# Sliding attention: the shift is added on the way to SBUF, and four exponentials become one

## The reference

```python
def swa_sink_attention(q, k, v, sinks):
    ...
    s = jnp.einsum('bcqhgd,bckhd->bchgqk', qc, kb, preferred_element_type=F32) * (D ** -0.5)
    s = jnp.where(valid[None, :, None, None, None, :], s, -jnp.inf)
    sink = sinks.astype(F32).reshape(1, 1, Hkv, G, 1, 1)
    m = jnp.maximum(jnp.max(s, axis=-1, keepdims=True), sink)
    e = jnp.exp(s - m)
    p = e / (jnp.sum(e, axis=-1, keepdims=True) + jnp.exp(sink - m))
    out = jnp.einsum('bchgqk,bckhd->bcqhgd', p.astype(v.dtype), vb)
    return out.reshape(B, S, Hq * D)
```

## Time and profile before

| what | value |
|---|---|
| median of 3 runs | 2261.44 us (2260.76 to 2262.36) |
| the profiled execution | 2261.36 us, its span 2259.6 us |
| mean granted clock of TensorE | 0.998 |
| busy share of the span | TensorE 99%, weight loads 83%, VectorE 78%, ScalarE 52%, GpSimd 37% |
| the stage with the 32 groups | about 1430 to 1600 us of the span |

### The profile page before, as it was taken

The page is one execution under the profiler, slowest core; times in us unless marked ns, Lnnn a source line. Parts: engine busy times, 40 slices in busy tenths (PEclk is TensorE's granted clock), DMA queues, the critical chain, the costliest instruction groups (busy, mean ns, idle before and its releaser), DMA issues. The chain is left out here.

```text
span 2259.6 us, 31830 instructions
## 1 busy us (share of the span) xinstructions
PE 2227.7 (99%) x11331; PEld 1885.4 (83%) x11331; DVE 1761.6 (78%) x2696; ACT 1183.0 (52%) x1951; POOL 840.1 (37%) x750
## 2 busy tenths in 40 slices
PE   7999999999999999999999999999999999999999
PEld 6888889999888888888888888888888888888887
DVE  5886789956557888888799767756598888888987
ACT  5658888766433444444445644655444444444454
POOL 3113346310001677777400022222048777871000
PEclk9999999999999999999999999999999999999999
DMA  5111100100322122222663542411322222228435
GB/s 169 36 50 47 34 33 29 39 1 1 140 103 75 66 84 84 84 84 84 222 216 103 181 139 61 107 39 57 112 66 84 84 84 82 82 70 303 154 118 199
DMA packets 190504, 215.18 MB, mean 95 GB/s; under 512 B 15524, under 2 KB 136708, under 8 KB 190348
## 3 DMA queue, kind: packets, MB, share of 16 engines
q1 hardware_dynamic: 185052, 195.81, 27.3%
q10 hardware_dynamic: 5296, 17.34, 2.0%
HBM read 170.77 MB, written 39.98 MB: 93 GB/s over the span
## 5 line engine op out<-in xcount | busy, mean ns | idle before, releaser
L123 PE MATMUL trunk_ps<-l_bhi,l_ahi 128*128 128x512 f32 x528 | 206.0, 390 | 0.5 <-DVE l_blo L3082 0.4
L123 PE MATMUL trunk_ps<-l_bhi,l_alo 128*128 128x512 f32 x528 | 205.5, 389 | 0.0
L123 PE MATMUL trunk_ps<-l_blo,l_ahi 128*128 128x512 f32 x528 | 205.4, 389 | 0.0
L123 PE MATMUL trunk_ps<-l_t_hi,l_s_hi 128*128 128x512 f32 x456 | 177.4, 389 | 0.0
L123 PE MATMUL trunk_ps<-l_t_hi,l_s_lo 128*128 128x512 f32 x456 | 177.4, 389 | 0.0
L123 PE MATMUL trunk_ps<-l_t_lo,l_s_hi 128*128 128x512 f32 x456 | 177.4, 389 | 0.0
L2698 POOL TENSOR_TENSOR l_s_lo<-l_raw,l_s_hi 128x512 fp32r<-128x512 f32 x90 | 158.1, 1765 | 45.5 <-ACT l_s_hi L2607 45.5
L2476 ACT ACTIVATE l_ahi<-l_a 128x512 fp32r<-128x512 f32 x132 | 83.2, 631 | 159.7 <-PE trunk_ps L123 151.2
L2698 POOL TENSOR_TENSOR l_s_lo<-l_w_sum,l_s_hi 128x512 fp32r<-128x512 f32 x76 | 120.4, 1586 | 56.6 <-ACT l_s_hi L2607 56.4
L216 POOL TENSOR_TENSOR wring_w_lo<-wring_raw,wring_w_hi 128x256 fp32r<-128x256 f32 x72 | 56.6, 817 | 191.8 <-ACT wring_w_hi L211 191.8
L123 PE MATMUL trunk_ps<-rest_hi,l_s_hi 128*128 128x512 f32 x304 | 118.3, 389 | 0.0
(11 more groups left out here) (495 smaller groups left out, 6722.6 us busy)
## 6 DMA issues: line engine op xcount, KB each, us to landing
l_draw<-in_ffn_w_out SPq DMA_DIRECT2D x154, 256.0 KB, 2.8
l_raw<-in_ffn_w_in SPq DMA_DIRECT2D x48, 512.0 KB, 4.6
gated_dram<-l_gate_out SPq DMA_DIRECT2D x44, 512.0 KB, 2.6
l_a<-gated_dram SPq DMA_DIRECT2D x88, 256.0 KB, 4.2
wring_raw<-in_even_w_in SPq DMA_DIRECT2D x20, 512.0 KB, 3.9
l_raw_g<-in_ffn_w_in SPq DMA_DIRECT2D x20, 512.0 KB, 3.9
l_raw_v<-in_ffn_w_in SPq DMA_DIRECT2D x20, 512.0 KB, 4.9
l_wt<-in_ffn_w_out SPq DMA_DIRECT2D x22, 256.0 KB, 6.0
```

The lines of the kernel that those rows point to most:

```text
L123: mm = pe.matmul(o, w, m, start=a, stop=z, skip_group_check=onto)
```

## The change

VectorE no longer leaves the scores in PSUM. Behind the shift it does one more operation in each group: scores + shift, for all four pairs at once, from S[n % 2] into prob[n % 2] (new semaphore `moved`). For that the shift is kept in the scores' own scale: `nbias` is now the smaller of -maximum and -8 x sink, with the new row `nsink8`, made by two small operations at the start. The exponent of the sink becomes 0.125 x nbias + sink, again one operation. ScalarE waits for `moved` and takes all four blocks' exponentials in one operation, prob into prob, with scale 0.125. Scores wait for `moved` where they waited for `exp_done`, and so does the feed-forward part's first product. The wait for `T_ready`, which guards prob, goes from ScalarE's exp to VectorE's move.

```diff
@@ -1084,13 +1086,8 @@
         def exp(n):
             nk = self.keys_of(self.where(n)[1])
-            sc.wait_ge(self.nb_ready, n + 1)
-            if n >= 2:
-                sc.wait_ge(self.T_ready, n - 1)
-            for u in range(self.PAIRS):
-                ins = sc.activation(self.prob[n % 2][:, u, 0:nk], self.S[n % 2][:, u * P:u * P + nk], ACT.Exp,
-                                    bias=self.nbias[:, n % self.ROWS, u:u + 1], scale=0.125)
-            ins.then_inc(self.exp_done, 1)
+            sc.wait_ge(self.moved, n + 1)
+            sc.activation(self.prob[n % 2][:, :, 0:nk], self.prob[n % 2][:, :, 0:nk], ACT.Exp, scale=0.125).then_inc(self.exp_done, 1)
@@ -1263,7 +1260,7 @@
             if n >= 2:
-                pe.wait_ge(self.exp_done, n - 1)
+                pe.wait_ge(self.moved, n - 1)
@@ -1381,13 +1378,18 @@
             dve.wait_ge(self.mx_ready, n + 1)
-            dve.scalar_tensor_tensor(out=self.nbias[:, n % self.ROWS, :], in0=self.mx[:, n % self.ROWS, :], scalar=-0.125,
-                                     in1=self.nsink[:, self.PAIRS * kv:self.PAIRS * kv + self.PAIRS], op0=ALU.mult, op1=ALU.min).then_inc(self.nb_ready, 1)
+            row, pairs, nk = n % self.ROWS, slice(self.PAIRS * kv, self.PAIRS * kv + self.PAIRS), self.keys_of(c)
+            dve.scalar_tensor_tensor(out=self.nbias[:, row, :], in0=self.mx[:, row, :], scalar=-1.0, in1=self.nsink8[:, pairs],
+                                     op0=ALU.mult, op1=ALU.min).then_inc(self.nb_ready, 1)
             dve.wait_ge(self.nb_ready, n + 1)
+            if n >= 2:
+                dve.wait_ge(self.T_ready, n - 1)
+            dve.tensor_tensor(self.prob[n % 2][:, :, 0:nk], self.S[n % 2].rearrange("p (u k) -> p u k", u=self.PAIRS)[:, :, 0:nk],
+                              self.nbias[:, row, :].rearrange("p (u c) -> p u c", c=1).to_broadcast([P, self.PAIRS, nk]), ALU.add).then_inc(self.moved, 1)
             if n >= self.ROWS:
                 dve.wait_ge(self.es_done, n - self.ROWS + 1)
-            dve.tensor_tensor(self.arg[:, n % self.ROWS, :], self.nbias[:, n % self.ROWS, :],
-                              self.nsink[:, self.PAIRS * kv:self.PAIRS * kv + self.PAIRS], ALU.subtract).then_inc(self.arg_ready, 1)
+            dve.scalar_tensor_tensor(out=self.arg[:, row, :], in0=self.nbias[:, row, :], scalar=0.125, in1=self.nsink[:, pairs],
+                                     op0=ALU.mult, op1=ALU.subtract).then_inc(self.arg_ready, 1)
@@ -1446,12 +1448,13 @@
             dve.tensor_scalar(self.nsink[half, :], self.sink[half, :, s], -1.0, None, ALU.mult).then_inc(self.sink_ready, 1)
+            dve.tensor_scalar(self.nsink8[half, :], self.sink[half, :, s], -8.0, None, ALU.mult).then_inc(self.sink_ready, 1)
...
-        dve.wait_ge(self.sink_ready, 2)
+        dve.wait_ge(self.sink_ready, 4)
@@ -2872,7 +2875,7 @@
-                    pe.wait_ge(odd.exp_done, odd.NG)
+                    pe.wait_ge(odd.moved, odd.NG)
```

More of the change, by code:

```diff
@@ L938, in __init__ @@
             at(x, [P] + rows, F32, small + 96 + 128 * i) for i, x in enumerate(("mx", "nbias", "arg", "es", "den", "inv")))
+        self.nsink8 = at("nsink8", [P, 8], F32, small + 864)
         self.ss, self.var, self.rstd = stats
@@ L956, in __init__ @@
             st.sem(x) for x in ("S_ready", "mx_ready", "nb_ready", "arg_ready", "exp_done", "es_done"))
+        self.moved = st.sem("moved")
         self.T_ready, self.copied, self.O_ready, self.den_ready, self.inv_ready, self.O_taken = (
```

## The result

The changed kernel takes 2269.64 us (median of six executions, 2263.76 to 2271.26), against 2261.02 (2259.51 to 2262.36) for the kernel before on the same chip: a ratio of 1.0035, with a 95% interval of 1.0022 to 1.0048. That is slower, and above the range of 2261.3 to 2266.4. The six executions are not alike. One took 2263.76, with a mean granted clock of 0.998, which is the forecast to 0.04 us; that close a hit is luck, since the six executions of the kernel before lie 2.85 us apart. The other five took 2269.04 to 2271.26, at 0.994 or 0.995. The profiled one is of the second kind: 2269.82 us, span 2268.0, mean clock 0.994.

The account below looks back on a forecast made before the run. TensorE, busy in 99% of the span, was taken to bound the kernel, with waits only in the sliding attention's head. Head delays of 0.8 + 1.1 + 0.5 = 2.4 us on 2261.4 gave 2263.8 us, range 2261.3 to 2266.4.

Parts of the forecast that it names:

- Step 1: Head, last queries: VectorE's moves of groups 0 and 1 delay the query packing and so scores 2; +0.8 us.
- Step 2: Head, group 2: VectorE's wait for the turned block delays the values' copy and TensorE's first product with them; +1.1 us.
- Step 3: Slots 3 to 5, no mixing between groups yet: longer path to the exponentials makes TensorE's turns late; +0.5 us.
- 2 us more of TensorE idle in the head: Sign in the profile after: less than this much added TensorE idle would show Step 3 failing.
- From slot 5 on, nothing: Later slots: mixing gives 3.1 us of cover against a 0.3 longer path; VectorE's load rises to 74%; no time added.
- The costs of single operations: Per group: VectorE's move taken at 0.69 us, ScalarE's joined exponential at 0.71 us against 1.14 for four.
- The sum of 2.4: Total shift from the head and slots 3 to 5: 0.8 + 1.1 + 0.5 us, giving 2263.8 us.
- the clock falls: Rival, head: TensorE's new holes lower the granted clock, costing 1.7 us more, 2265.5 us; chance 0.09.
- The long move: Rival, mainly head: VectorE's move doubles to 1.28 us, adding 3.0 us, 2266.8 us; chance 0.08.
- A head that swallows the shift: Rival, head: most of the delay vanishes, 2262.2 us, or 2260.5 at best; chance 0.10.
- The quicker stretch: Rival, TensorE's long stretch: it becomes quicker as ScalarE reads PSUM less beside it; chance 0.03.
- A granted clock below 1.00 around 1440 to 1450: Sign in the profile after, in the head, that would show the forecast wrong.

Follow-up runs that it names:

- own buffer: Changed kernel with a separate probability buffer for group 2, so VectorE's move need not wait for group 0's turn: 2263.04 us, ratio 1.0005.
- v_first: Changed kernel with VectorE's copies of the values placed ahead of group 2's maximum, shift and move: 2263.25 us, ratio 1.0005.
- second profile: Changed kernel, unaltered, in a second set of runs: median 2268.49 us, ratio 1.0029; the profiled execution took 2264.70 us.
- best order: Changed kernel with group 1's maximum, shift and move behind the last query packing, and values' copies earlier on VectorE and ScalarE: 2262.18 us, ratio 1.0000.
- four exponentials in place: v_first with four exponentials in SBUF, one per pair, instead of one for all four pairs: 2265.21 us, ratio 1.0011.

## Why the prediction was wrong, point by point

- **Step 1 (+0.8): right.** Measured +0.72. The packing of the last queries starts later by group 1's move, and scores 2 start at 1439.64, forecast 1439.6. It has a neighbour that I had left out, and that the change doesn't make: where the swapped rows landed later, the hole was 1.79 instead of 1.02.
- **Step 2 (+1.1): right.** Measured +1.21, through the wait named (VectorE 1.57 us for the turn, forecast about 1.5) and the product at 1444.73 (forecast 1444.55). The own buffer and v_first each took away that wait, and with it the 1.21.
- **Step 3 (+0.5): right in its place, a little large.** Measured +0.29 to +0.33 where the clock did not fall (11.54 to 11.58, against 11.25). The exponential was a mis-sized term, 0.63 us where 0.71 was taken. Group 3 shows it alone: from the start of its shift to its turn it takes 1.61 us (1448.58 to 1450.19, second profile), and 1.39 before (1445.60 to 1446.99), so +0.22 for a forecast +0.30. TensorE waits 0.61 us for group 4, and no longer for group 5, where the kernel before had 0.38 and 0.55; how the rest of the 0.2 divides was not taken apart. As a sign I had set 2 us more of TensorE idle in the head. The second profile has holes of 4.2 us (1.79, 1.45, 0.19, 0.61, 0.16), 2.7 more than the 1.47 of the earlier trace rows, but 0.8 of that is the late swapped rows; the first has only 2.47, as at the low clock TensorE no longer waits for the exponentials. The sign was a poor one.
- **From slot 5 on, nothing: right.** TensorE's waits in the kernel after, from 1436 to 1620 us (line, releaser: us in total, times, longest), are the two of the head and one at 1610 us, which the kernel before has too (at 1601.5):

```profile
PE trunk_ps L1292 <- DVE odd_v_even L1467: 1.4, 1, 1.4
PE trunk_ps L1267 <- DVE odd_q L142: 1.0, 1, 1.0
PE trunk_ps L123 <- ACT main_cos L1123: 0.8, 1, 0.8
```

  With the clock back, a slot is still 5.40 us. TensorE's turns, and VectorE's heaviest slot, the one with the norm, in the timeline of the kernel after (compare):

```profile
1509.46 0.62 PE L1279 MATMUL trunk_ps<-main_const,odd_prob 128*128 128x128 f32 x4
...
1514.86 0.62 PE L1279 MATMUL trunk_ps<-main_const,odd_prob 128*128 128x128 f32 x4
...
1509.66 0.69 DVE L1378 TENSOR_REDUCE odd_mx<-trunk_ps 128x4 f32<-128x512 f32 x1 [1.89 <-PE trunk_ps L1268]
...
1515.08 0.68 DVE L1378 TENSOR_REDUCE odd_mx<-trunk_ps 128x4 f32<-128x512 f32 x1
```

  That slot of VectorE takes 5.42 us from maximum to maximum (forecast 5.6), without a gap, and pushes nobody. VectorE was busy 70% of the stretch, forecast 74%: in a row of dense operations the next one starts 0.61 us behind a move (1511.22 behind 1510.61), so a move costs 0.61 there, not 0.69, and the kernel after comes to this stretch some 7.6 us later than before. The own buffer's stretch, with no long fall ahead of it, has 99.09 of 138, 72%.
- **The costs of single operations.** Move 0.691 us x30, forecast 0.69. Exponential 0.631, forecast 0.71. The Trainium skill (VectorE: DVE Perf Modes, section "The TRN2 errata") gave an estimated 0.61 for the latter; the trace has 0.63, closer to the page than my row was, and that row of 0.71 has a per-partition operand that this exponential no longer has. Since nothing from slot 5 on waits for it, the difference is worth little.
- **The sum of 2.4: right for what it added up.** The three steps come to 2.2 us where the clock is 1.00. The two executions at 0.998 took 2263.76 and 2264.70, forecast 2263.8, but of the two only the second was profiled, and its head was 3.0 us longer, not 2.2. That the times agree so well is in part luck.
- **The clock: this is the step that failed.** The sum of 2.4 had it at nothing, and the rival "the clock falls" had it wrong in its chance and in its price. I gave it 0.09. In 10 of the 14 executions of the changed kernel the mean clock was 0.995 or less. What I held against it, the 1.47 us of holes in today's head at a clock of 1.00, adds up holes of 0.24 to 0.55 us each, and none is near the 1.5 us that I had myself forecast. The one row on such a single hole, a longer one of 1.94 us, showed a fall. I had one row for, one sum against, and should not have gone below a half. The price, 1.7 us, was 4 us at 0.57, from a place where the clock was back at 1.00 from 584 us on. Here it stayed at 0.50 for 17 us, and the cost is 5.4 + 0.7 = 6.1 us: 2261.4 + 2.2 + 6.1 = 2269.7, the measured median. It is not the full half of 17 us. At the low clock TensorE no longer waits in slots 3 to 5 for the exponentials and for the bank O (0.80 and 0.16 us in the second profile); why the rest is not lost either was not looked into.
- **The other rivals.** The long move didn't happen (0.69). A head that swallows the shift didn't either. The quicker stretch: the slot is 5.40 with and without.
- **The sign.** "A granted clock below 1.00 around 1440 to 1450" stood among the signs that would show the prediction wrong, and it is what the profile shows.

The Trainium skill (TensorE: Matmul & The Clock Gate, section "Part 1: The HAM clock gate") says that a monitor on the chip sets TensorE's clock by how busy it has been lately. The traces agree as far as the 1.35 to 1.47 us holes ahead of each fall in the head go. In the second profile of the changed kernel the same hole had no fall behind it, so the hole makes a fall likely here and doesn't settle it.

## What to carry to other kernels

When a change moves a wait to an engine with a full queue, ask first what stands behind it there: here an order of three statements, or one more buffer, was worth 5 us, while the change's own work cost next to nothing (with the best order it is level with the kernel before). Price a new hole of TensorE twice, as the time it lasts and as the clock that may fall behind it, and take the second price from what TensorE does next: a long run of small matmuls can keep the low level for 15 us and more. A single execution is no verdict then: look at the mean clock of each, and remember that it shows long falls only.

## What the runs showed of the hardware

- The same program with the same holes ran its head at either clock level from one execution to the next: 2264 us or 2270 us. With its hole of 1.45 us, 10 of 14 executions had the mean clock of a long fall (0.995 or less). With the hole of 1.02 alone none of 22 had (own buffer, and v_first: 0.997 or more, and 1.00 in the head of both profiles); where longer waits in slots 4 and 5 came on top (four exponentials in place), one of 11 had 0.994.
- With the low level granted, TensorE was busy in each of 17 us, and the clock rose only 1.5 us after the matmuls of 512 columns had begun (1461.69). With eight such matmuls put ahead, it was back under 3 us after they had begun; with sixteen of 128 columns it was not. Behind a hole of 1.47 us it was back in less than 4 us with none of 512 columns.
- The exponential of 128x512 in place, without an operand per partition, takes 0.63 us, and 0.71 with such an operand; four of 128x128 take 0.91 in SBUF, and 1.14 from PSUM with the operand.
